# Expert bias products on two row groups of the array, in a two-layer diffusion and MoE step

## The chip, the core and the metric

The kernel runs on one core of one Trainium2 chip. The metric is the device time of one execution in microseconds (us), the median of several runs. Everything is computed in float32. Names used: PE is TensorE, DVE is VectorE, ACT is ScalarE, POOL is GpSimd, and SP is the engine that issues the weight loads.

## What is computed

One inference step of a backbone with two layers, for 128 context tokens and 128 latent tokens, of 1024 channels each. A layer has an adaptive modulation, a first sub-layer (latent attention, a gated linear recurrence, differential attention, merged by gates) and a second sub-layer, a mixture of 32 experts of which each token takes four. The change is in the second:

```python
combine = jnp.einsum('tk,tke->te', w_top, jax.nn.one_hot(top_i, N_EXPERTS))
def expert(acc, e):
    w1, b1, w2, b2, ce = e
    gu = t @ w1 + b1                       # b1: 1024 values for each expert
    gate = jnp.minimum(gu[:, :D_EXPERT], SWIGLU_LIMIT)
    up = jnp.clip(gu[:, D_EXPERT:], -SWIGLU_LIMIT, SWIGLU_LIMIT)
    act = (up + 1.0) * (gate * jax.nn.sigmoid(SWIGLU_ALPHA * gate))
    return acc + ce[:, None] * (act @ w2 + b2), None
```

The bias b1 is what the changed products add.

## The kernel before

The kernel is one loop over the two layers. At its end the engines clear the semaphores and meet (L1622, L1623), then branch back. Each engine has its own program; semaphores set the order between them.

The experts are computed in passes of two. Expert i of a pass owns 64 of the 128 rows of a block, filled with up to 64 of the tokens that chose it; an expert with more tokens gets a further turn. A pass on PE (`pair`, L793) is, in this order:

- L812: the gathered tokens times w1, in two parts of four chunks of 128 channels. The two experts are computed on two column groups of the array (`ps[c, h, :]` with c of 64 rows), and the results h = 0 and 1 (gate and up) go to banks 0 and 1 of PSUM, added to what is there (`start=False`).
- L771 (`gather`): one-hot products that gather the tokens of the next pass; L820 and L824: transposes.
- L837: activations times w2.
- L845: scatter back to the tokens.
- L778 (`biases`): writes the biases of the next pass into banks 0 and 1 (`start=True`), ahead of its L812. Each is a product of a one-hot `oh` (expert of each row, 32 partitions by 128) with the table `b1` (32 experts by 1024), one for h = 0 and one for h = 1, so both contract over partitions 0 to 31. `biases` is also called once ahead of pass 0 (L791). So there are 18 calls a layer.

DVE writes `oh` (L1505) and the other one-hots (L1503, L1514) for the pass after, in `tokens_onehot`, by comparing a constant column of partition numbers (C_PIDX) with the expert's number `eidf`, which stands in all partitions. In pass 0 it works on the routing first (L1480 to L1584). ACT loads the table at L1052 (helper `cache`, L884) by one DMA, long before the expert passes, then squares the residual as it comes (L1056). PE waits for the table at L789.

SP loads the weights (L405). A pass needs six parts of 2048 KB: slots 0 and 1 hold the first half of w1 for the two experts, slots 2 and 3 the second half, slots 4 and 5 w2. A slot is loaded again when PE has used it: SP waits for the first part of L812, the second part of it, and L837 in turn. Parts for the first passes go to spare places and are loaded ahead. In the last pass of layer 0 SP issues the first loads of layer 1 in the same way (L325: four of `ada_w`, two of `w_in`), then goes to the meeting of the engines. At the end of the last pass DVE adds the result to the residual (L1616), ACT squares it (L1094), and in layer 1 SP stores it (L474). The next layer's PE program begins with L493.

Two other places run two products side by side: L680 and L683, the scores of differential attention, where the two maps of a head contract over partitions 0 to 63 and 64 to 127 and go to banks 2 and 3:

```python
for c in range(2):
    r = slice(64 * c, 64 * c + 64)
    mm(ps[:, 2 + c, 0:128], b[r, 0:128], b[r, 256:384], start=True, stop=True)
```

and L812 and L837 with their column groups.

Of the kernel before, what the change touches and what calls it, by code (L numbers as in the profile page):

```python
# [20 lines left out]
ALU = mybir.AluOpType  # L21
# [3 lines left out]
P = 128  # L25
D = 1024
# [12 lines left out]
N_EXP, D_EXP, TOP_K = 32, 512, 4  # L39
SLOTS = 64  # L40
# [19 lines left out]
C_PIDX, C_KK, C_EIDX, C_EPS, C_FOLD = 704, 705, 721, 753, 754  # L60
# [34 lines left out]
def build(nc, x_in, cond_in, consts, vecs, rows, ada_w, w_in, w_q_b, w_kv_b, lru_gate_w, w_o_mla, w_o_lru,  # L95
# [3 lines left out]
    with ctx:  # L99
# [10 lines left out]
        cst = sb("cst", [P, NC])  # L110
# [31 lines left out]
        ps = ctx.enter_context(nc.psum_tensor("ps", [P, 8, 512], F32))  # L142

        def at(off, *dims):
            n = 1
            for d in dims:
                n *= d
            v = arena[:, off:off + n]
            if len(dims) == 2:
                return v.rearrange("p (a b) -> p a b", a=dims[0])  # L150
            if len(dims) == 3:
                return v.rearrange("p (a b c) -> p a b c", a=dims[0], b=dims[1])
            if len(dims) == 4:
                return v.rearrange("p (a b c d) -> p a b c d", a=dims[0], b=dims[1], c=dims[2])
            return v
# [10 lines left out]
        E0 = 8512  # L166
# [27 lines left out]


        more = [at(0, SLOT), at(SLOT, SLOT)]
        b1 = at(E0 + 2048, D)
        b2 = at(19776, D)
        X2 = at(E0, G, D)
        xTg = at(E0 + 3072, KC, P)  # L200
# [6 lines left out]
        oh = at(E0 + 8448, P)  # L207
# [16 lines left out]
        eidf = at(T0 + 758, NTAB)  # L224
# [16 lines left out]
        ld_rw, ld_b1, ld_b2 = sem("rw_in"), sem("b1_in"), sem("b2_in")  # L241
# [126 lines left out]
        with nc.Fori(0, L) as l:  # L368
            with nc.Block() as block:
# [115 lines left out]
                def _(pe):  # L485
                    mm = nc.tensor.matmul
# [78 lines left out]
                    for n, (kind, w) in enumerate((("tok", 512), ("tok", 160), ("feat", 512), ("feat", 512),  # L565
# [4 lines left out]
                        for half in range(2):  # L570
# [7 lines left out]
                            if kind == "tok":  # L578
                                for k in range(KC):
                                    if u == 0:  # L580
                                        pe.wait_ge(h_v[0], k + 1)
                                    if u == 1:
                                        pe.wait_ge(h_a[0], k + 1)
                                    last = mm(ps[:, bank, 0:w], hT[:, k, half * P:(half + 1) * P],  # L584
                                              slot[:, k, :], start=k == 0, stop=k == KC - 1)
                            else:
                                for c in range(2):
                                    for k in range(KC):
                                        ch = 2 * half + c
                                        last = mm(ps[:, bank, c * NT:(c + 1) * NT],  # L590
                                                  slot[:, k, ch * P:(ch + 1) * P], hT[:, k, :],
                                                  start=k == 0, stop=k == KC - 1)
# [70 lines left out]
                    for u in range(12):  # L663
# [8 lines left out]
                        if u < 8:  # L672
# [3 lines left out]
                               stop=True).then_inc(s_mm, 1)  # L676
                        else:
# [5 lines that stand above are left out]
                                last = mm(ps[:, 2 + c, 128:384], b[r, 128:256], b[r, 384:640], start=True,  # L683
                                          stop=True)
# [8 lines left out]
                        for n in range(3):  # L693
                            last = tr(ps[:, 4, n * P:(n + 1) * P], probs[u % 2][:, 0, n * P:(n + 1) * P], ident)
# [7 lines left out]
                        t = probsT[u % 2]  # L702
                        if u < 8:
                            if u % 2 == 0 and u:
                                pe.wait_ge(om_ev, u // 2)
                            r = slice(64 * (u % 2), 64 * (u % 2) + 64)
                            c = slice(u * VD, (u + 1) * VD)
# [3 lines left out]
                               stop=True).then_inc(pv_mm, 1)  # L711
                        else:
# [3 lines left out]
                            else:  # L716
                                pe.wait_ge(od_ev, u - 8)
                            c = slice((u - 8) * P, (u - 7) * P)
# [3 lines left out]
                               stop=True).then_inc(pv_mm, 1)  # L722
# [11 lines left out]
                    for k in range(KC):  # L734
                        pe.wait_ge(h_v[1], k + 1)
                        pe.wait_ge(h_a[1], k + 1)
                        c = slice(32 * (k % 4), 32 * (k % 4) + 32)
                        last = mm(ps[c, 1, 0:NT], rw[:, k, :], hT[:, k, :], start=k < 4, stop=k >= 4)  # L738
# [12 lines left out]
                    for g in range(G):  # L751
                        last = mm(ps[:, 1, 256 + g * N_EXP:256 + (g + 1) * N_EXP], lpart[:, g * P:(g + 1) * P],
                                  cst[:, C_FOLD:C_FOLD + N_EXP], start=True, stop=True)
# [21 lines left out]

                    def biases():
                        for h in range(2):
                            mm(ps[:, h, :], oh[0:N_EXP, :], b1[0:N_EXP, h * 512:(h + 1) * 512], start=True,  # L778
                               stop=True, skip_group_check=True)

                    pe.wait_ge(disp, 1)
                    pe.wait_ge(x2_ev, 4)
# [3 lines left out]
                    for g in range(G):  # L786
                        last = mm(ps[0:N_EXP, 0, g * P:(g + 1) * P], cmb[:, g, :], ident, start=True, stop=True)
                    last.then_inc(ct_mm, 1)
                    pe.wait_ge(ld_b1, 16)  # L789
                    pe.wait_ge(ct_ev, 1)  # L790
                    biases()  # L791

# [75 lines left out]
                def _(act):  # L868
# [14 lines left out]
                    def cache(dst, src, s):  # L883
                        act.dma_start(dst, src[bass.ds(l, 1), :, :].rearrange("o p n -> (o p) n")).then_inc(s, 16)  # L884
# [11 lines left out]
                    for j in range(2):  # L896

                        src = lru_gate_w[bass.ds(l, 1), bass.ds(j, 16, step=2), :, :]
# [55 lines left out]
                    for v in range(10):  # L954
# [5 lines left out]
                        else:  # L960
                            s = v // 2 - 2
                            src = ps[:, half, :].rearrange("p (h n) -> p h n", h=4)
# [60 lines left out]
                    for u in range(12):  # L1023
                        act.wait_ge(nm_v, u + 1)
                        j = u % 2
                        if u < 8:
                            for n, c in enumerate((slice(0, 128), slice(128, 384))):
                                last = A(probs[j][:, 0, c], ps[:, 2 + j, c], ACT.Exp, bias=nm[:, j, n:n + 1],
                                         accum_out=sums[:, j, n:n + 1])
                        else:  # L1030
                            for n, c in enumerate((slice(0, 128), slice(128, 384))):
                                for m in range(2):
                                    e = 2 * n + m
                                    last = A(probs[j][:, m, c], ps[:, 2 + m, c], ACT.Exp, bias=nm[:, j, e:e + 1],
                                             accum_out=sums[:, j, e:e + 1])
# [13 lines left out]

                    act.wait_ge(pv_mm, 12)  # L1050
                    act.wait_ge(out_done, 16 * 5)
                    cache(b1[0:N_EXP, :], exp_b1, ld_b1)  # L1052
                    cache(b2[0:N_EXP, :], exp_b2, ld_b2)
                    for k in range(KC):
                        act.wait_ge(f_dv, 24 + k + 1)
# [8 lines left out]
                    for g in range(G):  # L1064
                        last = A(exl[:, g, :], lgt[:, g, :], ACT.Exp, bias=nv1[:, g:g + 1])
# [32 lines left out]
                def _(dve):  # L1098
                    V = nc.vector
# [91 lines left out]
                    for g in range(G):  # L1191
# [4 lines left out]
                        last = V.tensor_tensor_reduce(out=spare[:, g, 384:640], in0=kv, in1=kv, scale=1.0, scalar=0.0,  # L1196
                                                      op0=ALU.mult, op1=ALU.add, accum_out=ss[:, 2 + g:3 + g])
# [4 lines left out]
                    for g in range(G):  # L1202
# [3 lines left out]
                        last = V.scalar_tensor_tensor(out=kv, in0=kv, scalar=ss[:, 2 + g:3 + g],  # L1206
                                                      in1=row[:, R_KVA:R_KVA + KV_LORA], op0=ALU.mult, op1=ALU.mult)
# [10 lines left out]
                    for j in range(4):  # L1218
                        for c in range(RC):
                            w = vec[:, V_CW + 4 * j + c:V_CW + 4 * j + c + 1]  # L1220
                            o = xr[:, c, :].rearrange("p (g n) -> p g n", g=G)
                            if j == 0:
                                last = V.tensor_scalar(o, xpad[:, c, :, 0:P], w, vec[:, V_CB + c:V_CB + c + 1],
                                                       ALU.mult, ALU.add)
                            else:
                                last = V.scalar_tensor_tensor(out=o, in0=xpad[:, c, :, j:j + P], scalar=w, in1=o,
                                                              op0=ALU.mult, op1=ALU.add)
# [81 lines left out]
                    for d in range(2):  # L1309
                        h = lru_h[d]  # L1310
# [187 lines left out]
                    def tokens_onehot(t):  # L1498

                        for i in range(2):  # L1500
                            c = slice(SLOTS * i, SLOTS * (i + 1))
                            for g in range(G):
                                V.tensor_scalar(S_s[:, g, c], cst[:, C_IOTA:C_IOTA + SLOTS],  # L1503
                                                pmT[:, g, bass.ds(t + i, 1)], None, ALU.is_equal)
                            last = V.tensor_scalar(oh[0:N_EXP, c],  # L1505
                                                   cst[0:N_EXP, C_PIDX:C_PIDX + 1].broadcast_to((N_EXP, SLOTS)),
                                                   eidf[0:N_EXP, bass.ds(t + i, 1)], None, ALU.is_equal)
                        return last

                    def combine_onehot(t):  # L1510
# [115 lines left out]
def constants(np):  # L1626

    c = np.zeros((P, NC), np.float32)
    c[:, C_ID:C_ID + P] = np.eye(P)
    c[:, C_UT:C_UT + P] = np.triu(np.ones((P, P)), 1)  # L1630
    c[:, C_ONE:C_ONE + P] = 1.0
    c[:, C_IOTA:C_IOTA + P] = np.tile(np.arange(SLOTS), 2)
    for dim, cc, cs in ((ROPE, C_CM, C_SM), (DH, C_CD, C_SD)):
        half = dim // 2
        inv = (1.0 / (np.float32(10000.0) ** (np.arange(0, half, 2, dtype=np.float32) / np.float32(half))))
        inv = inv.astype(np.float32)
        t = np.arange(P)
        ang = [((pos.astype(np.float32))[:, None] * inv[None, :]).astype(np.float32) for pos in (t // 64, t % 64)]
        ang = np.concatenate([ang[0], ang[0], ang[1], ang[1]], axis=1)
        sign = np.tile(np.repeat([-1.0, 1.0], half // 2), 2)  # L1640
        c[:, cc:cc + dim] = np.cos(ang)
        c[:, cs:cs + dim] = np.sin(ang) * sign
    c[:, C_PIDX] = np.arange(P)
    c[:, C_EPS] = EPS
    c[:, C_FOLD:C_FOLD + N_EXP] = np.tile(np.eye(N_EXP), (P // N_EXP, 1))
    c[:, C_KK:C_KK + MAX_EXTRA] = np.arange(MAX_EXTRA)
    c[:, C_EIDX:C_EIDX + N_EXP] = np.arange(N_EXP)
    return c
# [57 lines left out]
```

## Time and profile before

| | us |
|---|---|
| median of 3 runs | 1832.1 (1832.06 to 1835.03) |
| the profiled execution, first to last instruction | 1829.6 |
| PE busy | 1758.5 (96%) |
| PE weight loads busy (beside PE) | 1007.2 (55%) |
| DVE busy | 605.9 (33%) |
| ACT busy | 275.9 (15%) |
| L778, 144 records | 71.2 |
| read from HBM, MB | 548.31 |

The profile is of one execution. A "busy" time of PE includes matmuls whose ends are modelled, so a gap in its work shows better in the starts of its instructions than in the busy share. The chain of waits follows the work back from the last instruction to what released it; the time in it is what a change has to shorten. "Idle before, releaser" says what an engine waited for. A load's time to landing is from its issue to its last byte.

### The profile page before, as it was taken

How to read it: one execution, taken by the hardware profiler on the slowest of the kernel's cores; microseconds unless marked ns; L12 is line 12 of the kernel's file. 1: busy time of each engine (PE TensorE's matmuls, PEld its weight loads, DVE VectorE, ACT ScalarE, POOL GpSimd, SP SyncE). 2: the span in 40 equal slices, each digit the busy share in tenths (PEclk: the TensorE clock that was granted, in tenths of full speed). 3: DMA queues.
4: the chain of work that ended last, by engine and by line, in shares of the span. 5: the costliest groups of instructions: out<-in, count | busy, mean ns of one | idle time of the engine just before them, and what ended most of it. 6: DMA issues, size and time to landing. Idle time of an engine off the chain costs nothing.

```text
span 1829.6 us, 22228 instructions
## 1 busy us (share of the span) xinstructions
PE 1758.5 (96%) x8560; PEld 1007.2 (55%) x8560; DVE 605.9 (33%) x1733; ACT 275.9 (15%) x611; POOL 3.8 (0%) x6
## 2 busy tenths in 40 slices
PE   3999999989999999999979999998999999999998
PEld 1756787744444445454438468877445454444444
DVE  2377245261212122121233863543522121212122
ACT  2033222120000000000030422212100000000001
POOL 0000000000000000000000000000000000000000
PEclk9999999999999999999989999999999999999999
DMA  9754634957699999999975445368667999999994
GB/s 333 270 179 144 236 139 160 345 214 276 250 403 403 407 404 406 403 407 402 401 264 199 161 171 189 141 238 317 255 250 273 401 408 402 406 405 405 407 401 183
DMA packets 176492, 551.52 MB, mean 301 GB/s; under 512 B 12720, under 2 KB 15536, under 8 KB 176304
## 3 DMA queue, kind: packets, MB, share of 16 engines
q1 hardware_dynamic: 167408, 546.20, 77.7%
q10 hardware_dynamic: 9024, 4.53, 1.1%
q8 instruction: 36, 0.59, 0.1%
q14 instruction: 24, 0.20, 0.0%
HBM read 548.31 MB, written 2.40 MB: 301 GB/s over the span
## 4 chain that ended last, share of the span: by engine, by line
PE 47%; DVE 2%; issue 1%; ACT 0%; DVEq 0%; ACTq 0%
PE ps L812 12%; PE ps L623 8%; PE ps L837 7%; PE ps L771 4%; PE ps L584 3%; PE ps L845 3%; PE ps L778 2%; PE ps L590 2%; PE ps L502 1%; PE ps L820 1%; PE ps L560 1%; PE ps L493 1%; PE ps L555 0%; PE ps L521 0%; PE ps L738 0%
## 5 line engine op out<-in xcount | busy, mean ns | idle before, releaser
L812 PE MATMUL ps<-ring,arena 128*64 128x512 f32 x2112 | 460.6, 594 | 0.0
L812 PEld LDWEIGHTS ps<-ring,arena 128*64 128x64 f32 x2112 | 148.7, 137 | 307.6 <-issue 307.6
L837 PE MATMUL ps<-ring,arena 128*64 128x512 f32 x1088 | 241.0, 595 | 0.0
L623 PE MATMUL ps<-hT,ring 128*128 128x256 f32 x768 | 171.4, 379 | 0.0
L1514 DVE TENSOR_SCALAR arena<-cst,arena 128x64 f32<-128x64 f32 x136 | 33.4, 310 | 398.6 <-PE ps L812 398.6
L623 PEld LDWEIGHTS ps<-hT,ring 128*128 128x128 f32 x768 | 144.1, 190 | 19.4 <-issue 1.0
L837 PEld LDWEIGHTS ps<-ring,arena 128*64 128x64 f32 x1088 | 75.1, 137 | 141.6 <-issue 141.6
L771 PEld LDWEIGHTS ps<-arena 128*128 128x128 f32 x1152 | 134.0, 192 | 34.5 <-issue 26.0
L771 PE MATMUL ps<-arena 128*128 128x128 f32 x1152 | 143.7, 278 | 6.6 <-DVE arena L1505 6.6
L623 PE MATMUL ps<-arena,ring 128*128 128x256 f32 x640 | 144.6, 380 | 2.9 <-ACT arena L1020 1.6
L1079 ACT ACTIVATE arena<-arena 128x512 f32<-128x512 f32 x34 | 21.4, 630 | 779.0 <-DVE arena L1592 779.0
L623 PEld LDWEIGHTS ps<-arena,ring 128*128 128x128 f32 x640 | 118.8, 190 | 19.0 <-issue 2.7
L845 PE MATMUL ps<-arena 128*128 128x256 f32 x544 | 126.5, 386 | 0.0
L584 PE MATMUL ps<-ring,hT 128*128 128x512 f32 (+1 forms) x320 | 121.4, 540 | 1.9 <-DVE hT L1179 1.9
L845 PEld LDWEIGHTS ps<-arena 128*128 128x128 f32 x544 | 100.6, 190 | 39.9 <-issue 27.6
L1604 DVE COPY arena<-ps 128x512 f32<-128x512 f32 x34 | 23.5, 692 | 222.9 <-PE ps L837 222.9
L584 PEld LDWEIGHTS ps<-ring,hT 128*128 128x128 f32 x320 | 58.0, 192 | 63.8 <-issue 62.5
L1592 DVE TENSOR_SCALAR arena<-ps 128x512 f32<-128x512 f32 x34 | 23.5, 690 | 149.5 <-PE ps L812 149.5
L778 PE MATMUL ps<-arena 32*128 32x512 f32 x144 | 71.2, 613 | 1.1 <-ACT arena L1068 1.1
L493 PE MATMUL ps<-arena,cst 128*128 128x256 f32 x64 | 19.1, 465 | 38.3 <-PEq L334 28.0
L590 PE MATMUL ps<-hT,ring 128*128 128x256 f32 x256 | 55.6, 379 | 0.0
L590 PEld LDWEIGHTS ps<-hT,ring 128*128 128x128 f32 x256 | 48.5, 190 | 6.5
(266 smaller groups left out, 1303.0 us busy)
## 6 DMA issues: line engine op xcount, KB each, us to landing
ring<-exp_w_dram SPq DMA_DIRECT2D x194, 2048.0 KB, 12.3
ring<-ada_w_dram SPq DMA_DIRECT2D x24, 2048.0 KB, 9.3
ring<-w_in_dram SPq DMA_DIRECT2D x12, 2048.0 KB, 11.0
ring<-w_merge_dram SPq DMA_DIRECT2D x12, 2048.0 KB, 9.0
ring<-w_out_dram SPq DMA_DIRECT2D x4, 2048.0 KB, 10.8
arena<-exp_w_dram SPq DMA_DIRECT2D x4, 2048.0 KB, 18.1
ring<-w_o_lru_dram SPq DMA_DIRECT2D x2, 2048.0 KB, 7.8
ring<-w_o_mla_dram SPq DMA_DIRECT2D x2, 2048.0 KB, 19.6
```

Of the source, the lines that this page charges most:

```text
L493: last = mm(ps[:, bank, 0:NT], ones, sq[:, k, :], start=k == 0, stop=k == KC - 1)
L584: last = mm(ps[:, bank, 0:w], hT[:, k, half * P:(half + 1) * P], slot[:, k, :], start=k == 0, stop=k == KC - 1)
L590: last = mm(ps[:, bank, c * NT:(c + 1) * NT], slot[:, k, ch * P:(ch + 1) * P], hT[:, k, :], start=k == 0, stop=k == KC - 1)
L623: last = mm(out, slot[:, k, cols], src[:, k, :], start=k == 0, stop=k == nk - 1)
L771: last = mm(ps[:, 2 + k // 4, (k % 4) * P:(k % 4 + 1) * P], X2[:, g, k * P:(k + 1) * P], S_s[:, g, :], start=g == 0, stop=g == 1)
L778: mm(ps[:, h, :], oh[0:N_EXP, :], b1[0:N_EXP, h * 512:(h + 1) * 512], start=True, stop=True, skip_group_check=True)
L812: last = mm(ps[c, h, :], xTg[:, 4 * part + k, c], w[i][:, k, h * 512:(h + 1) * 512], start=False, stop=True, skip_group_check=True)
L837: last = mm(ps[c, 2 + h, :], actT[:, f, c], w[i][:, f, h * 512:(h + 1) * 512], start=f == 0, stop=f == 3)
L845: last = mm(ps[:, 4 + k // 2, (k % 2) * NT:(k % 2 + 1) * NT], O_s[:, k * P:(k + 1) * P], SCT[:, :], start=first and k % 2 == 0, stop=True, ...
L1514: V.tensor_scalar(SC_s[:, g, SLOTS * i:SLOTS * (i + 1)], cst[:, C_IOTA:C_IOTA + SLOTS], pmT[:, g, bass.ds(t + i, 1)], cwT[:, g, bass.ds(t ...
L1592: V.tensor_scalar(gate_s, ps[:, 0, :], LIMIT, None, ALU.min).then_inc(gate_v, 1)
L1604: V.tensor_copy(O_s[:, 512:1024], ps[:, 3, :]).then_inc(o_v, 1)
```

## The change

The table `b1` is split in two: its first 512 columns (gate) lie on partitions 0 to 31, the other 512 (up) on partitions 32 to 63, loaded by two DMAs. The one-hot `oh` is written on 64 partitions, the same values twice; for this the constant column C_PIDX counts modulo 32. The product for h = 0 contracts over partitions 0 to 31, that for h = 1 over 32 to 63.

```diff
-        b1 = at(E0 + 2048, D)
+        b1 = at(E0 + 2048, D_EXP)

                     def biases():
                         for h in range(2):
-                            mm(ps[:, h, :], oh[0:N_EXP, :], b1[0:N_EXP, h * 512:(h + 1) * 512], start=True,
-                               stop=True, skip_group_check=True)
+                            r = slice(N_EXP * h, N_EXP * (h + 1))
+                            mm(ps[:, h, :], oh[r, :], b1[r, :], start=True, stop=True, skip_group_check=True)

-                    pe.wait_ge(ld_b1, 16)
+                    pe.wait_ge(ld_b1, 32)

-                    cache(b1[0:N_EXP, :], exp_b1, ld_b1)
+                    for h in range(2):
+                        src = exp_b1[bass.ds(l, 1), :, h * D_EXP:(h + 1) * D_EXP]
+                        act.dma_start(b1[N_EXP * h:N_EXP * (h + 1), :],
+                                      src.rearrange("o e n -> (o e) n")).then_inc(ld_b1, 16)

-                            last = V.tensor_scalar(oh[0:N_EXP, c],
-                                                   cst[0:N_EXP, C_PIDX:C_PIDX + 1].broadcast_to((N_EXP, SLOTS)),
-                                                   eidf[0:N_EXP, bass.ds(t + i, 1)], None, ALU.is_equal)
+                            last = V.tensor_scalar(oh[0:2 * N_EXP, c],
+                                                   cst[0:2 * N_EXP, C_PIDX:C_PIDX + 1].broadcast_to(
+                                                       (2 * N_EXP, SLOTS)),
+                                                   eidf[0:2 * N_EXP, bass.ds(t + i, 1)], None, ALU.is_equal)

-    c[:, C_PIDX] = np.arange(P)
+    c[:, C_PIDX] = np.arange(P) % N_EXP
```

## Rows read from the trace of the kernel before

**Rows 1.** The page, busy tenths in 40 slices of the span, PE and DMA

```profile
PE   3999999989999999999979999998999999999998
...
DMA  9754634957699999999975445368667999999994
```

**Rows 2.** Chain of waits, one pass of layer 1: start us, us, engine, line, records

```profile
1382.96 3.65 PE ps L845 x16
1386.61 1.91 PE ps L778 x4
1388.52 13.88 PE ps L812 x64
...
1419.59 13.88 PE ps L812 x64
```

**Rows 3.** The page's costliest groups, and the line L778 (ns min/median/max, first and last start)

```profile
L1604 DVE COPY arena<-ps 128x512 f32<-128x512 f32 x34 | 23.5, 692 | 222.9 <-PE ps L837 222.9
...
L778 PE MATMUL ps<-arena x144: 587/587/692, 382.3 to 1822.9; 32*128 32x512 f32 x144
```

**Rows 4.** Windows: us, busy of PE, PEld, DVE, ACT, POOL, PEclk, DMA share, GB/s

```profile
1371.00:1402.00 31.00, 31.00 (x156) 14.62 (x154) 6.69 (x17) 2.21 (x4) 0.00 (x0) 1.00 0.56 199
...
1433.00:1451.00 18.00, 18.00 (x96) 10.31 (x94) 4.75 (x7) 2.21 (x4) 0.00 (x0) 1.00 1.02 412
1464.00:1482.00 18.00, 18.00 (x96) 10.31 (x94) 4.75 (x7) 2.21 (x4) 0.00 (x0) 1.00 1.03 410
```

**Rows 5.** Timeline around L778: start us, us, engine, line, operands, records, idle before

```profile
1386.54 0.29 PEld L778 LDWEIGHTS ps<-arena 32*128 32x128 f32 x2 [0.33 <-issue]
...
1387.08 0.18 PEld L778 LDWEIGHTS ps<-arena 32*128 32x128 f32 x1 [0.24 <-issue]
...
1388.45 0.20 PEld L812 LDWEIGHTS ps<-ring,arena 128*64 128x64 f32 x4 [0.76 <-issue]
```

**Rows 6.** Timeline, PE at the scores of differential attention, layer 1

```profile
1200.18 0.49 PE L680 MATMUL ps<-arena 64*128 64x128 f32 x4
1200.51 0.60 PE L683 MATMUL ps<-arena 64*128 64x256 f32 x4
1201.04 0.48 PE L623 MATMUL ps<-arena,ring 128*128 128x256 f32 x1
```

**Rows 7.** Waits of PE: us in total, times, longest

```profile
PE ps L771 <- DVE arena L1505: 6.6, 4, 1.8
```

**Rows 8.** Timeline, end of layer 1

```profile
1819.07 4.23 DVE L1616 SCALAR_TENSOR_TENSOR xT<-ps,modT,xT 128x128 f32<-128x128 f32 x16 [0.36 <-PE ps L845]
```

**Rows 9.** Fourth load of a pass: its issue, and us from issue to landing

```profile
1403.15 0.37 SPq L405 DMA_DIRECT2D ring<-exp_w_dram  x1
...
ring<-exp_w_dram SPq DMA_DIRECT2D x1, 2048.0 KB, 15.9
```

**Rows 10.** Timeline, SP at the end of layer 0

```profile
895.13 11.95 SPq L325 DMA_DIRECT2D ring<-ada_w_dram  x4
913.62 4.49 SPq L325 DMA_DIRECT2D ring<-w_in_dram  x2
```

**Rows 11.** Timeline, ACT and PE at the end of layer 0

```profile
915.84 3.52 ACT L1094 ACTIVATE arena<-xT 128x256 f32<-128x256 f32 x7
...
929.43 1.19 PE L493 MATMUL ps<-arena,cst 128*128 128x256 f32 x2 [10.29 <-issue]
```

**Rows 12.** Windows, between the layers

```profile
920.00:925.00 5.00, 0.00 (x0) 0.00 (x0) 0.00 (x0) 0.00 (x0) 1.80 (x1) 0.69 1.06 387
```

**Rows 13.** One-hot and bias table: lines L1505 and L884, and ACT's timeline behind them

```profile
L1505 DVE TENSOR_SCALAR arena<-cst,arena x72: 235/236/240, 376.6 to 1801.5; 32x64 f32<-32x64 f32 x72
...
L884 ACTq DMA_DIRECT2D arena<-exp_b_dram x4: 369/376/384, 315.8 to 1220.9; - x4
...
335.89 0.42 ACT L1056 ACTIVATE arena<-xT 128x256 f32<-128x256 f32 x1 [19.63 <-DVE xT L1392]
```

**Rows 14.** DMA queues, GB/s in 40 slices of 1402 to 1433

```profile
GB/s 418 423 423 412 402 402 418 418 412 418 407 396 402 423 412 412 423 386 402 418 418 412 418 391 402 412 423 407 418 418 386 407 418 412 248 206 407 375 412 423
```

## The prediction

> **What bounds the kernel now.** I read the 40 slices of the page first [rows 1]: TensorE (PE) is at nine tenths or more nearly everywhere, and from slice 12 to 20 and 32 to 39 so are the DMA engines. Two resources are full at the same time, so the question is which one ends last. The chain of waits answers it for the expert loop [rows 2]: it lies on PE alone, from the first L812 of a pass (1388.52) to that of the next (1419.59), 31.07 us, without a wait. The page has 34 of L1604, which is run once a pass [rows 3], so there are 34 passes, 17 a layer. The bias products of a pass, L778, take 1.91 us of it [rows 2].
>
> The DMA engines are just behind. A pass loads six parts of 2048 KB, 12.58 MB. Where the queue never runs dry they move 410 to 412 GB/s [rows 4], which makes 30.5 to 30.7 us a pass; I take 30.65. So the loads are idle for only 0.4 us of 31.07, and any gain above that per pass makes the loads the slower side.
>
> **What changes on PE.** A product in f32 is two records here (144 records for 36 calls of two products [rows 3]). The four of a call start one after another: 1.91 us is 4 x 0.43, and 0.2 at entry and exit for weight loads that nothing hides [rows 2, 5]. The change puts the two products on rows 0 to 31 and 32 to 63 of the array, into different banks. The nearest row is the differential attention, L680 and L683: two products on rows 0 to 63 and 64 to 127, also into two banks. From their first start to the next weight load are 0.86 us for four records of 128 columns and four of 256 [rows 6]. A 256-column record costs 0.22 when it runs alone (16 in 3.65 with the way in, [rows 2]), so eight in a row would cost 4 x 0.11 + 4 x 0.22 = 1.3, plus 0.2; in pairs 0.66 plus 0.2 = 0.86. They ran in pairs, both halves of each product. L812 shows the same for column groups: 64 records of 512 columns in 13.88 us [rows 2] is 0.217 each, two at a time. So the call should take two slots in place of four: 1.91 - 2 x 0.43 = 1.05, and 0.85 saved. Bounds: -0.6 (a loss, below) to +0.86.
>
> No row shows groups of 32 rows. The Trainium skill (TensorE: Matmul & The Clock Gate, "Packing small matmuls") says that products on different row groups run concurrently, and gives 3.07 times for four of 32 rows and 512 columns. Scaled to two that would be an estimate of some 0.6 saved instead of 0.85; the rows on L680 and L683 speak for the larger value, and no run yet shows the 32-row case.
>
> **Which calls count.** Each layer has 18 calls: one ahead of pass 0 and one at the end of each pass. The first is hidden: in pass 0 PE waits for DVE's routing chain anyway (the four waits of L771 for L1505, 6.6 us in total, two of them here [rows 7]), and that chain doesn't hang on the biases. The last feeds nothing: in layer 1 the output follows from L845 through L1616, which began at 1819.07 [rows 8], while the last record of L778 starts at 1822.9 [rows 3]. Sixteen remain, 16 x 0.85 = 13.6 us a layer if nothing else binds.
>
> **The loads in layer 1.** From the fourth pass on (1388) the queue is full: the DMA share is 0.56 in the stretch up to 1402 and 1.02 and 1.03 after it [rows 4], and stays at nine tenths to the last slice but one [rows 1]. That is the loads for 13 passes. PE alone would go at 31.07 - 0.85 = 30.22, the loads at 30.65. That does not stop PE at once, since parts land before they are needed. The tightest is the fourth of a pass: issued at 1403.15, landed 15.9 later at 1419.1 [rows 9], needed in the second half of L812, at 1419.59 + 6.94 = 1426.5. Slack 7.5 us. It shrinks by 0.43 a pass, 5.6 us over 13 passes, and some 1.9 us are left. So layer 1 keeps its whole 13.6; at 30.8 a load-pass in place of 30.65 the slack would just be used up. Price of that: zero to 1 us.
>
> **The loads in layer 0.** Here the backlog has to be paid. After the last pass SP issues the next layer's ada_w and w_in loads and is held in the issue itself: the last two issues take 4.49 us [rows 10], against 0.37 for one that isn't held [rows 9]. It comes free at 918.11 (913.62 + 4.49), which I take to go with the progress of the queue and not with PE. Just behind it ACT ends, at 919.36 (915.84 + 3.52 [rows 11]); then all engines meet. With the change ACT and PE are 13.6 earlier, 905.8. The queue is earlier only by what starts it earlier, the calls of passes 0 to 2, 3 x 0.85 = 2.55, and by the idle time taken out of it, 12 or 13 x 0.4 = about 5.0: 7.6 us. SP would be free at 910.5 and end last. Layer 0 gains 919.36 - 910.5 = 8.8; I take 0.4 off for a longer stall behind the meeting: PE stands still until 929.43, and the queue still moves 387 GB/s in the meantime [rows 11, 12], and I cannot tell from these rows how much of that is the queue. So 8.4, between 3.8 (no idle time is won back: 2.55 + 1.25) and 13.6 (SP isn't held).
>
> The Trainium skill (DMA: Bandwidth & Descriptors, "Queues, rings and completion order") says an engine serves its queues in turn, packet by packet. By it the stall would stay about as long as now, not grow with the backlog; no row separates the two.
>
> **The other edits.** The bias table comes as two DMAs of 64 KB instead of one of 128: one more issue of 0.38 us on ACT [rows 13], whose next work (L1056) waits 19.63 us after it; PE needs the table at 382.3, 66 us later. Zero; without that idle time 0.4 a layer. The one-hot write L1505 goes from 32 to 64 partitions, at 236 ns now [rows 13]. I take it as unchanged; twice that, two a pass, would still lie beside PE, since the chain has no DVE in a pass [rows 2]. C_PIDX and the semaphore's 32: zero.
>
> **Sum.** 13.6 + 8.4 = 22.0 us. The profiled span of 1829.6 becomes 1807.6; the median of before is 2.5 above its span, so 1810.1.
>
> **Rivals.**
> (a) The queue's idle time can't be won back, since each set of loads begins with a start-up gap whatever is queued (the dip to 248 and 206 GB/s once a pass [rows 14] would be that). Layer 0 gains 3.8; in layer 1 the backlog is 13 x 0.85 = 11.1 against 7.5, so 13.6 - 3.6 = 10.0. Total 13.8: 1818.3. Against it: a pass begins three sets of loads, and that row has one dip.
> (b) Products start in strict order, and the second record of the first product goes ahead of the second product: three slots, 0.43 saved. Pass 30.64, just the pace of the loads; 16 x 0.43 x 2 = 13.8, 1818.3 too. L680 and L683 would then take 0.86 + 0.2 = 1.05, and they take 0.86 [rows 6]. The Trainium skill (TensorE: Matmul & The Clock Gate, "The mechanism") states that matmuls start and end in program order; taken for the records, that gives this rival.
> (c) No overlap of 32-row groups: 1832, within 0.2%.
> (d) Slower: every hop between row groups drains and reloads as the way in and out of L778 does (0.2 us for both together [rows 5]), without overlap. Three hops in a call are 0.6 us, 16 x 0.6 x 2 = 19, 1851. It decides as soon as the overlap gives back less than the hops cost. L680 and L683 speak against it.
> (e) SP isn't held and the stall doesn't grow: 13.6 a layer, 1804.9.
>
> **How the numbers follow.** Forecast 0.63, (a) 0.12, (b) 0.08, (c) 0.08, (d) 0.04, (e) 0.05. The forecast's own range is 1807 to 1814. The range of 1804 to 1820 takes in (e), (a) and (b), and leaves out (c) and (d). About 0.2% (3.7 us) is what a measurement of this kernel can tell from no change. Faster: 0.63 + 0.12 + 0.08 + 0.05 = 0.88, less 0.02 for a mix of (c) with a small gain: 0.86; same 0.09; slower 0.05.
>
> **What the profile after would show.** L778: from its first start to L812's weight load 1.05 instead of 1.91, starts in pairs. A pass of 30.2 us in both layers, without an idle time ahead of L812's second half; if that appears in the last passes, the slack was smaller. The dip in the GB/s once a pass gone, the fourth part's landing later each pass. At the end of layer 0 SP's last issue ends after ACT, with PE idle ahead of the next L493 for longer than the 10.29 us of now [rows 11]. Wrong would be: starts of L778 0.43 apart, or a pass near 31.07 with PE idle ahead of L812 (the loads hold it).

## The result, and the profile after

The kernel with the change took 1814.7 us, the median of 4 runs (1811.05 to 1816.68), against 1832.08 (4 runs, 1829.52 to 1835.03). The ratio is 0.990, with an interval of 0.9887 to 0.9918: 17.4 us less, where 22.0 were forecast; the time is inside the range of 1804 to 1820, and 0.7 above the forecast's own 1807 to 1814. The profiled execution has a span of 1813.4 against 1829.6.

A pass of the changed kernel, in its chain of waits (start us, us, engine, line, records); L779 is L778 of before:

```profile
1442.75 1.06 PE ps L779 x4
1443.81 13.88 PE ps L812 x64
1457.69 2.88 PE ps L771 x24
...
1462.31 7.02 PE ps L837 x32
1469.32 3.65 PE ps L845 x16
1472.97 1.06 PE ps L779 x4
1474.03 6.15 PE ps L812 x27
```

From 1443.81 to 1474.03 is 30.22 us, where [rows 2] have 31.07. Every entry is as before but one: the bias call takes 1.06 in place of 1.91. The weight loads of that call (start, us, count):

```profile
1442.68 0.30 PEld L779 LDWEIGHTS ps<-arena 32*128 32x128 f32 x4 [0.33 <-issue]
1443.74 0.20 PEld L812 LDWEIGHTS ps<-ring,arena 128*64 128x64 f32 x4 [0.76 <-issue]
```

All four are done within 0.30 us, where [rows 5] have them spread over more than 1 us. PE's own records of this call start in pairs, two at 1442.68 and two at 1443.21: the two products run side by side.

The loads have lost their idle time. First the GB/s of one pass in 40 slices, then the fourth load of the last pass of layer 1, its issue and its time to landing:

```profile
GB/s 396 407 423 418 402 412 407 402 418 418 402 407 418 396 412 423 407 407 412 402 407 418 412 402 412 412 402 412 418 407 412 407 402 412 418 412 402 412 407 402
```

```profile
1760.66 3.54 SPq L405 DMA_DIRECT2D ring<-exp_w_dram  x1
```

```profile
ring<-exp_w_dram SPq DMA_DIRECT2D x1, 2048.0 KB, 22.1
```

The dip of [rows 14] is gone. The fourth load took 15.9 us to land in [rows 9] and takes 22.1 here. It landed at 1782.8, and the last pass, whose L812 begins at 1776.25, needed it at 1783.2: 0.4 us of slack are left. PE did not wait for a load anywhere.

Then pass 0 of layer 1, which the forecast had not looked into. Chain of waits, the gather behind PE's wait for DVE, and what follows; under it the same lines of the kernel before:

```profile
1299.98 4.57 PE ps L771 x24
...
1316.77 1.06 PE ps L779 x4
1317.83 3.78 PE ps L858 x16
1321.61 15.20 PE ps L812 x64
```

```profile
1304.15 2.94 PE ps L771 x24
...
1321.22 3.45 PE ps L858 x16
1324.68 15.58 PE ps L812 x64
```

The same 24 records of L771 take 4.57 us in place of 2.94. The granted clock in the windows of the gather of pass 0 in layer 0 (the columns are those of [rows 4]; the clock is the third from the end), changed kernel and before:

```profile
402.90:407.10 4.20, 4.20 (x24) 4.20 (x25) 2.52 (x4) 1.23 (x2) 0.00 (x0) 0.63 1.01 400
```

```profile
399.80:402.60 2.80, 2.79 (x25) 2.79 (x26) 2.54 (x4) 1.23 (x2) 0.00 (x0) 1.00 1.01 407
```

0.63 on average is a stretch at half clock (1.2 GHz) and a rest at full (2.4 GHz). Ahead of it PE has waited longer. The waits of L771 (us in total, times, longest), and the gather of pass 0 in layer 0 with the wait in brackets, changed kernel and before:

```profile
PE ps L771 <- DVE arena L1508: 8.3, 4, 2.5
```

```profile
402.89 4.43 PE L771 MATMUL ps<-arena 128*128 128x128 f32 x24 [2.48 <-DVE arena L1508]
```

```profile
399.81 2.94 PE L771 MATMUL ps<-arena 128*128 128x128 f32 x24 [1.63 <-DVE arena L1505]
```

In layer 1 the wait in pass 0 is 2.21 us, where it was 1.38. The 1.8 in [rows 7] is another wait, at the gather ahead of pass 0; it is the same in both kernels. The bias call ahead of pass 0 is done 0.85 us earlier, DVE's chain is not, and so the wait in pass 0 is 0.85 longer in each layer.

Last, the end of layer 0: SP's issues, the first work of POOL behind the meeting, and PE's first product of layer 1:

```profile
887.77 17.94 SPq L325 DMA_DIRECT2D ring<-ada_w_dram  x4
906.26 10.23 SPq L325 DMA_DIRECT2D ring<-w_in_dram  x2
```

```profile
920.12 1.80 POOL L481 MEMSET arena<- 128x2048 f32 x1 [890.65 <-POOLq L1627]
```

```profile
926.42 4.18 PE L493 MATMUL ps<-arena,cst 128*128 128x256 f32 x9 [15.49 <-issue]
```

SP is held until 916.49 in its issues, 4.5 us beyond ACT's end at 912.0, and PE's idle time ahead of L493 has grown from 10.29 [rows 11] to 15.49 us.

### The profile page after: what moved, and what is told of

It is laid out like the page before. It is cut to its first block, busy times and chain, and to the rows that moved or that the text cites. A ratio compares the mean times of both kernels' runs of the same rounds, so it can differ in the third digit from the quotient of the medians.

```text
span 1813.4 us, 22234 instructions
## 1 busy us (share of the span) xinstructions
PE 1734.7 (96%) x8560; PEld 999.6 (55%) x8560; DVE 606.5 (33%) x1733; ACT 275.5 (15%) x611; POOL 3.8 (0%) x6
## 4 chain that ended last, share of the span: by engine, by line
PE 47%; DVE 2%; issue 1%; ACT 0%; DVEq 0%; ACTq 0%
PE ps L812 12%; PE ps L623 8%; PE ps L837 7%; PE ps L771 4%; PE ps L584 3%; PE ps L845 3%; PE ps L590 2%; PE ps L502 1%; PE ps L779 1%; PE ps L820 1%; PE ps L560 1%; PE ps L493 1%; PE ps L555 0%; PE ps L521 0%; PE ps L738 0%
## 5 line engine op out<-in xcount | busy, mean ns | idle before, releaser
L812 PE MATMUL ps<-ring,arena 128*64 128x512 f32 x2112 | 460.6, 594 | 0.0
L812 PEld LDWEIGHTS ps<-ring,arena 128*64 128x64 f32 x2112 | 148.8, 137 | 307.6 <-issue 306.0
L771 PEld LDWEIGHTS ps<-arena 128*128 128x128 f32 x1152 | 138.7, 197 | 36.2 <-issue 26.0
L771 PE MATMUL ps<-arena 128*128 128x128 f32 x1152 | 148.5, 284 | 8.3 <-DVE arena L1508 8.3
L845 PE MATMUL ps<-arena 128*128 128x256 f32 x544 | 126.5, 386 | 0.0
L845 PEld LDWEIGHTS ps<-arena 128*128 128x128 f32 x544 | 100.5, 190 | 39.9 <-issue 27.6
L493 PE MATMUL ps<-arena,cst 128*128 128x256 f32 x64 | 20.2, 486 | 43.3 <-PEq L334 27.9
L999 ACT ACTIVATE arena<-ps,bmh 128x256 f32<-128x256 f32 x48 | 22.7, 473 | 142.4 <-PE ps L623 137.2
## 6 DMA issues: line engine op xcount, KB each, us to landing
ring<-w_in_dram SPq DMA_DIRECT2D x12, 2048.0 KB, 10.4
```

The source lines that it names most:

```text
L493: last = mm(ps[:, bank, 0:NT], ones, sq[:, k, :], start=k == 0, stop=k == KC - 1)
L771: last = mm(ps[:, 2 + k // 4, (k % 4) * P:(k % 4 + 1) * P], X2[:, g, k * P:(k + 1) * P], S_s[:, g, :], start=g == 0, stop=g == 1)
L812: last = mm(ps[c, h, :], xTg[:, 4 * part + k, c], w[i][:, k, h * 512:(h + 1) * 512], start=False, stop=True, skip_group_check=True)
L845: last = mm(ps[:, 4 + k // 2, (k % 2) * NT:(k % 2 + 1) * NT], O_s[:, k * P:(k + 1) * P], SCT[:, :], start=first and k % 2 == 0, stop=True, ...
L999: A(tg[:, ch, :], merge_ps(f), ACT.Tanh, bias=bmh[:, 8 * b + ch:8 * b + ch + 1], scale=0.5).then_inc(f_ac, 1)
```

## The experiments

Each kernel ran on one chip with the kernel before beside it. The first four were to tell whether the half clock in pass 0 comes from the change.

**The changed kernel once more.** No edit.

> The changed kernel once more, unchanged, beside the others on the same chip. Its pass should be 30.22 us as before. The first profile of it had TensorE at half clock for 3.41 us behind the wait of L771 in pass 0 of both layers, which the kernel before had not. If that follows from the change, it is there again in both layers, and the time is 1813 to 1816. If it was an accident of that one execution, it is gone and the time is 1810 to 1812.

Measured: 1813.5 us (1812.98 to 1815.16), before 1831.83 (17 runs), ratio 0.990 (0.9881 to 0.9915). The slow gather is there again; its window in layer 0 has a clock of 0.61:

```profile
401.80:406.20 4.40, 4.37 (x24) 4.37 (x25) 2.56 (x4) 1.23 (x2) 0.00 (x0) 0.61 1.01 398
```

In layer 1 the wait is 2.21 and the gather takes 4.49. So it is not an accident of one execution.

**First call on one row group.** The table is held with all its columns on both groups, and the call ahead of pass 0 uses one of them:

```diff
-                    def biases():
+                    def biases(split):
                         for h in range(2):
-                            r = slice(N_EXP * h, N_EXP * (h + 1))
-                            mm(ps[:, h, :], oh[r, :], b1[r, :], ...)
+                            g_ = h if split else 1
+                            r = slice(N_EXP * g_, N_EXP * (g_ + 1))
+                            mm(ps[:, h, :], oh[r, :], b1[r, h * 512:(h + 1) * 512], ...)
...
-                    biases()          # ahead of pass 0
+                    biases(False)
```

> Only the bias call ahead of pass 0 is put back on one row group (both products on partitions 32 to 63; the table has all 1024 columns on both groups for this); the calls at the end of the passes stay on two. The call ahead of pass 0 then takes 1.91 again in place of 1.05. Theory (the packed first call only lengthens PE's wait for DVE in pass 0, from 1.65 to 2.5 us, and the clock drops behind the longer wait): the wait is 1.65 again, the half clock of 3.41 us at the gather of pass 0 is gone in both layers, and the kernel is 1.7 us per layer faster than the changed one, about 3.4 in all, though it does more work. Rival (the drops come by chance or from elsewhere): they stay, and the time is that of the changed kernel to 1 us.

Measured: 1806.49 us (1806.38 to 1806.83), ratio 0.986 (0.9841 to 0.9873); 7.0 us less than the changed kernel beside it, where 3.4 were expected. Waits of PE, then the chain in pass 0 of layer 1:

```profile
PE ps L771 <- DVE arena L1510: 6.6, 4, 1.8
```

```profile
1295.05 2.94 PE ps L771 x24
...
1311.26 3.45 PE ps L860 x16
1314.71 13.88 PE ps L814 x64
```

The waits are as in [rows 7] again (in pass 0 1.65 us in layer 0 and 1.38 in layer 1), the gather takes 2.94, and L814 (L812) of pass 1 takes 13.88, where it took 15.20 in the changed kernel and 15.58 in the kernel before. So a kernel that keeps PE occupied longer is faster, and the second drop of the clock, at the start of pass 1, went with it in this layer. In layer 0 that one stayed: the granted clock from 421 to 424 is 0.56.

One thing speaks against reading this as a rule about the length of a wait. Ahead of pass 0, behind a wait of 1.8 us that is the same in all kernels, the gather of layer 1 ran at half clock here and at full clock in the kernel before:

```profile
1271.25 5.47 PE L771 MATMUL ps<-arena 128*128 128x128 f32 x32 [1.79 <-DVE arena L1510]
```

```profile
1281.99 3.84 PE L771 MATMUL ps<-arena 128*128 128x128 f32 x32 [1.78 <-DVE arena L1505]
```

It was slow like this in six of the ten executions profiled.

**Only the first call on two row groups.** The reverse: `biases(True)` ahead of pass 0, `biases(False)` at the end of each pass.

> The other half of the same question: only the call ahead of pass 0 is on two row groups, the 17 calls at the ends of passes of each layer use one. Passes take 31.07 again. Theory: PE's wait in pass 0 is 2.5 us, half clock follows behind it, and the kernel is 1.7 us a layer slower than the kernel before, some 3.4 us, 1835. Rival: no difference from the kernel before, 1832.

Measured: 1829.2 us (12 runs, 1827.55 to 1834.36), ratio 0.9987 (0.9977 to 0.9997): 2.6 us less than before, neither the 1835 nor the 1832. The chain of pass 0 in layer 1:

```profile
1301.81 4.57 PE ps L771 x24
...
1318.60 0.42 PE ps L780
1319.02 0.22 PE ps L860
1319.23 0.22 PE ps L780
...
1322.26 15.58 PE ps L814 x64
```

The part that was tested came as the theory said: the longer wait in pass 0 (2.47 and 2.21 us) and the gather at 4.57. What was not foreseen: the call at the end of pass 0 uses partitions 32 to 63 in this kernel, the b2 products right behind it (L860) use 0 to 31, and their records alternate. From 1318.60 to L814 at 1322.26 are 3.66 us, where L778 and L858 of before take 1.91 + 3.45 = 5.36. That gives back 1.7 us a layer, about what the clock costs, and hides that cost in the total. That the profiled execution is 2.4 us shorter than that of the kernel before comes from a stretch that the edit doesn't touch: from L493 of layer 1 to the first bias call are 354.2 us here and 357.5 there, where more of it ran at half clock. The records decide, not the total.

**First call three times.** In place of a slower call, more of it:

```diff
-                    biases()          # ahead of pass 0
+                    for _ in range(3):
+                        biases()
```

> The changed kernel with the call ahead of pass 0 made three times, the same values each time (3 x 0.95 + 0.2, some 3.0 us in place of 1.05, into the time that PE would wait for DVE). Theory: the wait of L771 in pass 0 falls from 2.5 to about 0.5 us, no half clock behind it, and the kernel is 3.4 us faster than the changed one; if the shorter wait also saves the drop at the start of pass 1, up to 7. Rival: the added products cost their 1.9 us a layer, 3.8 us slower than the changed kernel.

Measured: 1808.15 us (1806.7 to 1809.61), ratio 0.987 (0.9852 to 0.9886), 5.4 less than the changed kernel. The four waits are 4.8 us together, those in pass 0 are 0.76 and 0.50. The gather of pass 0 runs at full clock in both layers, and so does pass 1 in layer 1; in layer 0 the drop at pass 1 stayed.

```profile
1294.81 2.94 PE ps L771 x24
...
1314.48 13.88 PE ps L813 x64
```

It is another way to shorten the wait in pass 0, with the same effect: what counts there is how long PE waits, not how the first call is made.

The next four ask where the gain comes from and what limits it.

**All edits, but one row group.** `g_ = 0` for every call; the table is held with all its columns on both groups.

> All edits of the change (two DMAs for the table, here with all 1024 columns on both groups of partitions, the one-hot on 64 partitions, the constant modulo 32), but both products of every call contract on partitions 0 to 31. Theory (the whole gain is the overlap of the two row groups, and the other edits cost nothing): L778's four records start 0.43 us apart again, a pass is 31.07, the time is that of the kernel before, 1832 within 2 us. Rival (a part of the gain comes from the other edits, or they cost something that the overlap hides): more than 2 us off.

Measured: 1833.69 us (10 runs), before 1832.28 (15 runs), ratio 1.0002 (0.9993 to 1.0012). The other edits cost nothing that can be measured; the call takes 1.91 again:

```profile
1451.36 1.91 PE ps L780 x4
1453.27 13.88 PE ps L814 x64
```

**No bias call in the passes.** The biases of all passes but the first are left out.

> The changed kernel without the bias call at the end of the passes; only the one ahead of pass 0 is left. The biases of all other passes are left out. PE's own pass is 30.22 - 1.05 = 29.17 us. Theory (the loads take 6 x 5.12 = 30.72 a pass and cannot go faster): passes of 29.17 until the slack of some 7 us is used up at 1.55 a pass, from the eighth or ninth pass on 30.72 with PE waiting for the fourth load; against the changed kernel only 3.15 us in layer 0 and 3.5 in layer 1 are won, 1807. Rival (the loads can follow at a higher rate): 29.17 throughout, 33 x 1.05 = 35 us less, 1779.

Measured: 1804.17 us (1802.94 to 1805.45), ratio 0.985 (0.9835 to 0.9865). PE's waits, and the chain of waits late in layer 1:

```profile
PE ps L812 <- DMA ring<-exp_w_dram: 23.1, 18, 1.3
```

```profile
1594.46 22.77 DMA ring<-exp_w_dram
...
1617.37 7.10 PE ps L812 x32
...
1625.18 22.77 DMA ring<-exp_w_dram
...
1648.09 7.10 PE ps L812 x32
```

The chain now goes through the loads: from 1617.37 to 1648.09 is 30.72 us. The 33 calls counted in the expectation were 35 us of PE's work, and the time went down by 9 to 10. That is 3 more than the 6.7 expected; the drop at pass 1 of layer 1 lasts 3.4 us in this execution and 6.8 in the changed kernel's second one, which is 1.7 of it, and the rest I did not follow further. The loads have a floor of 30.72 a pass; the changed kernel at 30.22 is already below it and lives on its slack.

**The w_in loads behind the meeting.** On the kernel with the first call on one row group:

```diff
+                    with sp_.If(l > 0):
+                        ...
+                        for slot in (4, 5):
+                            load_early(sp_, this, slot)
...
-                        for slot, (s, v) in enumerate(freed(n_extra + N_EXP // 2)):
+                        for slot, (s, v) in enumerate(freed(n_extra + N_EXP // 2)[:4]):
```

> The kernel with the first call on one row group, and SP issues the two w_in loads of layer 1 (slots 4 and 5) after the engines have met instead of before; the four ada_w loads stay. In the profile of the changed kernel SP is held by the queue in its last issue until 916.55, while ACT was done at 912.03. Theory (SP's hold sets the meeting, and the stall behind it doesn't depend on how much is queued): the meeting is 4.6 us earlier, the stall is 6.3 us as before, time 1806.5 - 4.6 = 1802. Rival (the stall ends when the queue has run out, whatever the meeting): no gain, 1806 to 1807.

Measured: 1800.08 us (median of 5 runs, 1798.94 to 1806.22), ratio 0.984 (0.9821 to 0.9852); 6.4 less than the kernel it is built on by the medians, 3.9 by the ratios (they did not run beside each other), with 4.6 expected. POOL's first work and PE's first product behind the meeting:

```profile
908.05 1.80 POOL L489 MEMSET arena<- 128x2048 f32 x1 [878.45 <-POOLq L1637]
```

```profile
913.87 6.04 PE L501 MATMUL ps<-arena,cst 128*128 128x256 f32 x16 [10.32 <-issue]
```

```profile
915.26 1.80 POOL L481 MEMSET arena<- 128x2048 f32 x1 [885.39 <-POOLq L1629]
```

```profile
921.72 6.08 PE L493 MATMUL ps<-arena,cst 128*128 128x256 f32 x16 [15.56 <-issue]
```

The first two rows are this kernel's, the last two those of the kernel it is built on. POOL begins at 908.05 in place of 915.26, and PE 5.8 us after it (6.5 without the edit, 6.3 in the changed kernel, 6.6 in the kernel before). Of the 7.2 us at POOL 3.1 came before, since the last pass begins at 872.8 in place of 875.9: the first bias call began 1.3 earlier, and the drop at pass 1 of layer 0, worth 1.7, is missing in this execution. 4.1 are the meeting, which ACT now sets, at 900.58 + 4.03, while SP's last issue ahead of it ends at 898.7. So SP's hold had set the meeting. The stall behind the meeting was 6.3 us with the longer queue of the changed kernel and 6.6 before, so nothing shows it growing with the queue. In layer 0 PE waited once for a load here, 0.2 us: the slack is used up.

**With the b2 products beside the call of pass 0.** `biases(not first)` at the end of a pass, so that only the call of pass 0 uses partitions 32 to 63 for both products.

> As the kernel with late w_in loads, and the call at the end of pass 0 uses partitions 32 to 63 for both products, which lets it run beside the b2 products behind it (partitions 0 to 31), as it did by accident in the kernel with only the first call on two groups: there the two together took 3.68 us, here after a packed call 0.96 + 3.54. Theory: 0.8 us a layer less than the kernel with late w_in loads, of which layer 0 keeps only what the loads allow; 1.0 to 1.6 us faster than it. Rival: no difference.

Measured: 1799.79 us (1798.39 to 1800.36), ratio 0.982 (0.9807 to 0.9834). The records alternate as they did above:

```profile
1304.06 0.42 PE ps L788
1304.48 0.22 PE ps L868
1304.70 0.22 PE ps L788
```

1.0 to 1.6 us were expected, and the 0.3 against the kernel with late w_in loads is within the spread of the two: the total shows nothing. The stages do. From the first bias call of layer 1 to the end are 526.4 us, where the kernel with late w_in loads has 527.3, so the overlap is worth its 0.8 in this layer; the profiled execution reached its first bias call of layer 0 2.0 us later than the other one, which hides it. It is the fastest of the kernels run, 32.5 us below the kernel before.

## Why the prediction was right in kind and too high in size

**The overlap: right.** 0.85 saved a call was the forecast, 1.91 to 1.06 is measured, from a row on groups of 64 rows; groups of 32 behave alike. With both products on one group the gain is nil, so it is the overlap alone. The strict-order rival (b) falls, since the records start two and two, and so do (c) and (d). The Trainium skill (TensorE: Matmul & The Clock Gate, "Packing small matmuls") gives 3.07 times for four groups, from which I had an estimate of 0.6; the trace has 0.85.

**Where the gain arose.** The total alone proves little, since (a) and (b) at 1818.3 lay in the range too. The stages of the profiled executions tell more (us, from the starts in the timelines; "first call" is the bias call ahead of pass 0):

| kernel | (A) first call of layer 0 begins | (B) from it to L493 of layer 1 | (C) from there to the first call of layer 1 | (D) from there to the end |
|---|---|---|---|---|
| before | 382.35 | 547.08 | 357.51 | 542.66 |
| changed | 385.40 | 541.02 | 356.34 | 530.64 |
| changed, second execution | 384.35 | 539.57 | 355.38 | 532.20 |
| first call on one group | 383.76 | 537.96 | 356.11 | 527.37 |

The gain of layer 0 shows in B, that of layer 1 in D. The forecast had 8.4 and 13.6 for them; the changed kernel has 6.1 and 12.0. The change touches A and C only by one more load of the table.

**The loads in layer 1: right.** The slack was to shrink by 0.43 a pass to some 1.9 us; it shrank to 0.4. In the pass of [rows 9] the changed kernel starts from 6.4 us in place of 7.5 (issued at 1398.00, landed 16.1 later, needed at 1420.5), and from there it lost 0.50 in each of 12 passes, since a load pass is 30.72 and not 30.65. Rival (a) falls: the idle time was won back in full.

**The loads in layer 0: right in kind.** SP ended last, as said, and the gain was cut there; rival (e) falls. Forecast was a wait of PE longer than 10.29; it is 15.49. That the difference of 5.2 equals 13.6 less 8.4 is luck: counted from the first bias call of the layer, the last L845 ended 10.4 us earlier and not 13.6, L493 began 6.1 earlier and not 8.4, both for the reason below, and the wait is counted from the end of the last bias call, which is 0.85 shorter. With the first call back on one group the stage gained 9.1, against a forecast of 8.8 without the longer stall. That SP's hold is the cause was a reading of mine; the kernel with late w_in loads shows it. The 0.4 for a longer stall was not needed: 6.3 us behind the meeting against 6.6. The Trainium skill (DMA: Bandwidth & Descriptors, "Queues, rings and completion order") gives queues their turns packet by packet, from which I took that the stall would not grow; the stall in the trace did not, but no run tests the rule itself.

**The first call: here the sum failed.** The prediction says "The first is hidden", at a price of zero. Hidden it is, but what hides it is a wait, and the wait grew from 1.63 to 2.48 us in layer 0 and from 1.38 to 2.21 in layer 1. Behind it the clock went to half.

- Layer 1: L771 costs 1.63 more, and 13.6 - 1.63 is the 12.0 measured. L858 takes 0.33 more and the L812 behind it 0.38 less; that is one drop, which the kernel before has too, starting a little earlier.
- Layer 0: L771 costs 1.49 more (4.43 against 2.94). The drop at pass 1 is also twice as long in this execution, 1.69 us more from L858 to the end of L812; in the second execution it is as in the kernel before, so that part is not shown to be the change's. Both lie ahead of the passes in which the queue is full, so they delay the loads as well, and the stage gains 6.1 in place of 8.4; in the second execution it gains 7.5.

Both gathers ran at full clock as soon as the wait was short again, by a slower call or by more calls. I named the cover and did not ask what a longer wait does. Putting the first call back gave 7.0 us: 3.2 are the two gathers, and 3.3 the drop at pass 1 of layer 1, which lasts 6.8 us in the changed kernel beside it and is missing there. That drop is in the kernel before too, at 3.4 us (L812 at 15.58 us against 13.88), so layer 1 gains 15.3 there, 1.7 beyond the 13.6, for a reason that the prediction does not have.

**What one profile can't tell.** The two profiled spans differ by 16.2 us, the medians by 17.4. Up to the first call of layer 0 the changed kernel has 385.40 and 384.35 us and the kernel before 382.35, but 382.46 is reached by the kernel with late w_in loads, which has the split table and the wide one-hot too. From L493 to the first call of layer 1 the ten executions have 354.2 to 357.5, with different lengths at half clock. So 3 us of a span can be neither credited to the change nor charged to it.

## What to carry to other kernels

Two small products on different row groups of the array took 1.06 us here in place of 1.91; look for the same between neighbouring calls too, as with b2. Before costing a saved step at nothing because a wait hides it, look at how long that wait becomes: here it was worth more to keep the engine busy than to let it finish early. And where an engine is just ahead of the loads, work out the slack of the tightest load and over how many passes it lasts; a gain larger than the loads' idle time can be kept whole for as long as the slack holds.

## What the runs showed of the hardware that was not expected

- In pass 0 the granted clock fell to half behind PE's waits of 2.2 to 2.5 us, in both layers of all four executions that had them (the changed kernel twice, the ones with only the first call on two groups and without the calls in the passes), and did not behind the waits of 0.5 to 1.65 us there, in both layers of the other six. The stretch was some 3.4 us long (0.61 on average over 4.4) and cost 1.4 to 1.6 us in the gather. The length of a wait is not the whole condition: at the gather ahead of pass 0 of layer 1, behind 1.8 us, the clock was half in six executions and full in four. Why that differs, and why a further drop comes some 20 us after the gather of pass 0, at the start of pass 1, in some executions and not in others, stays open.
- Products of 32 rows run beside each other as those of 64 do, and also when they belong to different calls with 512 and 256 columns: 3.66 us in place of 5.36.
- Parts of 2048 KB land 5.12 us apart on average when the queue never runs dry (30.72 us for six), and SP is held in the issue when the queue is long: 10.23 us for the last two loads of layer 0 in the changed kernel, 1.02 for the same two issued behind the meeting.
